# The last down-projection block by thirds of the tokens, with the final norm of finished tiles between its matmuls

## The chip, the cores and the metric

One core of one Trainium2 chip runs the whole program in one launch. The metric is the device time of that core in microseconds; lower is better. Engines are named as in the profile: PE is TensorE, PEld its weight loads, DVE VectorE, ACT ScalarE, POOL GpSimd, SP the queue that issues the DMAs.

## The reference, cut to what matters

One layer of a decoder trunk on 1024 prompt tokens and 8 sample sequences of 4 tokens, all in fp32: two token mixers, then a SwiGLU feed-forward, then a last RMSNorm. The end of it is what the change touches:

```python
h2 = _rmsnorm(x, g_norm2) * (1.0 + scale2) + shift2
ffn = (jax.nn.silu(h2 @ w_ffn_gate) * (h2 @ w_ffn_up)) @ w_ffn_down
x = x + gate2 * ffn
...
y_prompt = _rmsnorm(xp, g_final)
y_sample = _rmsnorm(xs, g_final)
```

x has 1056 rows (tokens) of 1024, w_ffn_gate and w_ffn_up are 1024 x 2816, w_ffn_down is 2816 x 1024. gate2 is one vector for the prompt and one for each of the 8 sample sequences.

## The kernel before, in words

**Layout.** Through the feed-forward phase (`ffn_phase`, from line 1436) everything stands turned: X is 128 partitions x 8 groups of channels (n) x 1056 tokens. The 1056 tokens go by thirds of 352 (`span(c)`, c = 0 to 2), one PSUM bank each. The prompt fills tokens 0 to 1023, the samples the last 32.

**Precision.** Each fp32 matrix is split in a hi and a lo part, and a product is three matmuls: hi by hi, hi by lo, lo by hi. Activations are split when they are made. A weight is loaded into `raw` (SP, line 1613), ScalarE copies the hi part (`hi`, line 1726), GpSimd subtracts it for the lo part (`lo`, line 1795). These go by halves through rings of four slots: half k waits for its load, and for its slot to be used up (`s_used`, three halves back), and tells TensorE by `s_lo`.

**Blocks.** The 2816 inner channels go in 11 blocks of 256. A block has a "proj" step (gate and up) and a "down" step. `run` (line 1520) puts them in order: proj 0, then in a loop proj and down in turn, each down one block behind, and last down of block 10 by itself. So the last two steps are down 9 and down 10. A down step has four halves of weights. Halves 0 and 1 are the two groups of 128 inner channels for output channels n = 0 to 3, halves 2 and 3 the same for n = 4 to 7. Before the first 12 pieces TensorE waits for halves 0 and 1, before the other 12 for 2 and 3:

```python
for nh in range(2):
    sl = []
    for f in range(2):
        s, _, before = pl.half(2 * nh + f)
        pe.wait_ge(s_lo, before + 1)
        sl.append(s)
    for r in range(12):
        n, c = r // 3, r % 3
        bnk, turns = pl.piece(12 * nh + r)
        wait(pe, s_pf[bnk], turns)
```

A piece is one n and one third c: six matmuls of 352 columns (line 1675) into one of banks 0 to 3, which take turns. The step counts itself used (`s_used`) when its piece 11 or 23 is done, both halves at once. All four slots of the rings are in use in a down step, so half k of one down step stands in the slot of half k of the down step ahead of it where no proj lies between, as for blocks 9 and 10.

**Updates.** VectorE adds each piece to X (`add_prompt`, line 1912: X + gate2 * bank, 352 columns, or 320 for the last third) and frees the bank (`s_pf`). For the last third the 32 sample columns come first, in two small operations (`samples`, lines 1920 and 1923).

**The end.** When the last piece is in X, nine token tiles (eight of 128 tokens, one of 32) are turned back, normed and stored. Tile t: eight transposes into two banks (line 1717, TensorE), two squares with a sum over the row (line 1783, ScalarE), the mean square (lines 1957 and 1958, VectorE), the root (line 1787, ScalarE), the reciprocal and two products with g_final (`rows_out`, lines 1929 and 1935, VectorE) into one of four row buffers, and a store (line 1621 or 1623, SP). The eight banks make four pairs, so tile t waits for the products of tile t - 4. ScalarE's order is written out: the squares of tile t, then the root of tile t - 1. VectorE's is the mean square of tile t, then the products of tile t - 1. Roots use a table of ScalarE's, which is loaded ahead of the first of them (ACT_TABLE_LOAD).

Of the kernel before, what the change touches and what calls it, by code (L numbers as in the profile page):

```python
# [9 lines left out]
ALU = mybir.AluOpType  # L10
ACT = mybir.ActivationFunctionType


P = 128
D = 1024
# [13 lines left out]
EPS = 1e-6  # L29
# [1406 lines left out]
def ffn_phase(nc, g, a, loops=True):  # L1436

    with ExitStack() as ctx:
# [124 lines left out]

        def wait_full(e, kind, pl, k):

            if kind == "down":
                nh, r = k // 12, k % 12
                if r == 11:
                    e.wait_ge(s_used, pl.half(2 * nh + 1)[2] + 1)
                else:  # L1570
                    e.wait_ge(s_piece, pl.full(11 * nh + r) + 1)
            else:
                t, c = k // 3, k % 3
                if c == 2:
                    e.wait_ge(s_used, pl.half(2 * t + 1)[2] + 1)
                else:
                    e.wait_ge(s_piece, pl.full(2 * t + c) + 1)

        MISC = g.ps[4:8]
        ENDB = g.ps[4:8] + g.ps[0:4]  # L1580
        NE = len(ENDB) // 2
        PARTS = [(0, 512), (512, 512), (SEQ, NS)]
        seqv = lambda v: v.rearrange("p (b t) -> p b t", t=SLEN)

        with nc.Block() as block:
# [43 lines left out]
            def _(pe):  # L1629
# [24 lines left out]
                def step(kind, b, par, pl):  # L1654
                    if kind == "out":
                        tile3(pl, 0, mix=(b == 0))
                    elif kind == "proj":
                        for t in range(4):
                            tile3(pl, t, first=(t == 0 and isinstance(b, int) and b == 0))
                    elif kind == "down":  # L1660
                        pe.wait_ge(s_al, b * 6 + 6)
                        for nh in range(2):
# [9 lines that stand above are left out]
                                c0, w = span(c)  # L1672
                                for f in range(2):
                                    for m, (x, y) in enumerate(((Wh, Ah), (Wh, Al), (Wl, Ah))):
                                        last = pe.matmul(g.ps[bnk][:, 0:w], x[:, sl[f], n, :], y[:, par, f, c0:c0 + w],  # L1675
                                                         start=(f == 0 and m == 0), stop=(f == 1 and m == 2))
                                if r == 11:
                                    last.then_inc(s_used, 2)
                                else:
                                    last.then_inc(s_piece, 1)  # L1680
                    elif kind == "norm2":

                        pe.wait_ge(s_sq, KC - 1)
                        pe.wait_ge(s_sql, 1)
                        pe.wait_ge(s_cc, 2)
                        for b, (c0, m) in enumerate(PARTS):
                            pe.matmul(MISC[b][0:1, 0:m], g.ones[:, 0:1], SQ[:, c0:c0 + m], start=True, stop=False)  # L1687
                            pe.matmul(MISC[b][0:1, 0:m], g.ones[:, 0:1], SG[:, c0:c0 + m], start=False, stop=True).then_inc(s_row, 1)  # L1688
                        pe.wait_ge(s_rowc, len(PARTS))
                        for t in range(NT):  # L1690
                            n = P if t < NC else NS
                            last = pe.transpose(MISC[3][0:n, 64 + 2 * t:65 + 2 * t], TH[0:1, t * P:t * P + n], g.ident[0:1, 0:1])
                        last.then_inc(s_sum, 1)

                        pe.wait_ge(s_rd, 1)
                        for b, (c0, m) in enumerate(PARTS):
                            n = P if b < 2 else NS
                            pe.matmul(MISC[b][:, 0:m], g.ones[0:n, :], SQ[0:n, c0:c0 + m], start=True, stop=True).then_inc(s_rb, 1)  # L1698


                for half_ in range(2):
                    for k in range(4):
                        kk = 4 * half_ + k
                        last = pe.transpose(MISC[half_][0:KEEP, k * P:(k + 1) * P], g.pk[:, kk, :], g.ident[:, :])
                pe.transpose(MISC[2][0:H * NCOND, 0:P], g.nout[:, :], g.ident[:, :]).then_inc(s_co, 1)
                run(pe, step)

                lastp = Place(LOOP, None, 0)
                bnk, turns = lastp.piece(23)
                pe.wait_ge(s_pf[bnk], turns + 1)  # L1710
                for t in range(NT):
                    n = P if t < NC else NS
                    for b in range(2):
                        if t >= NE and b == 0:
                            pe.wait_ge(s_fo, t - NE + 1)
                        for k in range(4):
                            last = pe.transpose(ENDB[2 * (t % NE) + b][0:n, k * P:(k + 1) * P], X[:, 4 * b + k, t * P:t * P + n], g.ident[:, :])
                        last.then_inc(s_ft, 1)

            @block.scalar  # L1720
            def _(act):
# [54 lines left out]
                for t in range(NT + 1):  # L1776
                    n = P if t < NC else NS
                    for b in range(2):
                        if t < NT:
                            act.wait_ge(s_ft, 2 * t + b + 1)  # L1780
                            if 2 * t + b:
                                act.wait_ge(s_fs, 2 * t + b)
                            act.activation(TH[0:n, 0:512], ENDB[2 * (t % NE) + b][0:n, :], ACT.Square,  # L1783
                                           accum_out=fss[0:n, t, b:b + 1]).then_inc(s_fs, 1)
                    if t:
                        act.wait_ge(s_fm, t)
                        act.activation(fss[:, t - 1, 2:3], fss[:, t - 1, 2:3], ACT.Sqrt).then_inc(s_fr, 1)
# [52 lines left out]
            def _(dve):  # L1840
# [3 lines left out]
                def step(kind, b, par, pl):  # L1844
# [37 lines left out]
                    elif kind == "proj":  # L1882
                        for f in range(2):
# [7 lines left out]
                            for c in range(NPC):  # L1891
                                c0, w = span(c)
                                bnk, _ = pl.piece(6 * f + 3 + c)
                                gb, gt = pl.piece(6 * f + c)
                                wait_full(dve, "proj", pl, 6 * f + 3 + c)
                                dve.wait_ge(s_pf[gb], gt + 1)
                                wait(dve, s_al, n - 3 + (c + 1))
                                dve.scalar_tensor_tensor(AC[:, c0:c0 + w], SG[:, c0:c0 + w], 0.5, g.ps[bnk][:, 0:w],  # L1898
                                                         ALU.mult, ALU.mult).then_inc(s_pf[bnk], 1)
                    else:  # L1900
                        for k in range(24):
                            n, c = 4 * (k // 12) + k % 12 // 3, k % 3
# [12 lines left out]
                def samples(kind, pl, k, n, vec, count):  # L1915
# [6 lines left out]
                    dve.wait_ge(s_stm, count * 2 - 1)  # L1922
                    dve.tensor_tensor(X[:, n, SEQ:T], X[:, n, SEQ:T], stm[:, :], ALU.add).then_inc(s_stm, 1)

                def rows_out(t):

                    n = P if t < NC else NS
                    dve.wait_ge(s_fr, t + 1)
                    link(dve.reciprocal(fss[:, t, 3:4], fss[:, t, 2:3]))
                    if t == 0:  # L1930
                        dve.wait_ge(s_out, 16 * 4)
                    if t >= NXR:
                        dve.wait_ge(s_y[t % NXR], 16 * (t // NXR))
                    for b in range(2):
                        ins = dve.scalar_tensor_tensor(OT[0:n, t % NXR, 512 * b:512 * b + 512], ENDB[2 * (t % NE) + b][0:n, :], fss[0:n, t, 3:4],  # L1935
                                                       GF[0:n, 512 * b:512 * b + 512], ALU.mult, ALU.mult)
                    ins.then_inc(s_fo, 1)

# [10 lines left out]
                    dve.wait_ge(s_mh, m + 1)  # L1949
                    dve.tensor_tensor(g.Hl[:, m, :], mixed(m), g.Hh[:, m, :].bitcast(F32), ALU.subtract).then_inc(s_mlv, 1)  # L1950
                run(dve, step)
                dve.wait_ge(s_gf, 16)
                for t in range(NT + 1):
                    if t < NT:
                        n = P if t < NC else NS
                        dve.wait_ge(s_fs, 2 * t + 2)
                        link(dve.tensor_tensor(fss[0:n, t, 2:3], fss[0:n, t, 0:1], fss[0:n, t, 1:2], ALU.add))
                        dve.tensor_scalar(fss[:, t, 2:3], fss[:, t, 2:3], 1.0 / D, EPS, ALU.mult, ALU.add).then_inc(s_fm, 1)
                    if t:
                        rows_out(t - 1)  # L1960


class Shared:
# [68 lines left out]
```

## Time and profile before

| | |
|---|---|
| median of three runs | 2223.32 us (2222.83, 2223.32, 2227.84) |
| span of the profiled execution | 2216.5 us |
| its own time | not listed apart; the median is 6.8 us above the span, the fastest run 6.3 |
| PE busy | 2073.8 us, 94% |
| DVE, ACT, POOL busy | 37%, 26%, 27% |
| mean granted clock of PE | 0.959 |
| last down step's first matmul | at 2169.24 us |
| last piece's update of X ends | at 2193.29 us |
| first products for y | at 2198.80 us |

Times inside the profile are microseconds from the first instruction. In the timeline's rows a start and a length stand first, then the engine and the line, the operation with the tile that it writes and those it reads, the shapes, and how many of such are merged; a bracket names the idle time ahead and what ended it. In the windows view each stretch has its length, then the busy time of each engine with its count of instructions, then PEclk, the granted clock of TensorE as a share of 2.4 GHz, the share of the DMA engines and GB/s. The chain is the work that ended last, followed back from the end.

### The profile page before, as it was taken

How to read it: one execution, taken by the hardware profiler on the slowest of the kernel's cores; microseconds unless marked ns; L12 is line 12 of the kernel's file. 1: busy time of each engine (PE TensorE's matmuls, PEld its weight loads, DVE VectorE, ACT ScalarE, POOL GpSimd, SP SyncE). 2: the span in 40 equal slices, each digit the busy share in tenths (PEclk: the TensorE clock that was granted, in tenths of full speed). 3: DMA queues.
4: the chain of work that ended last, by engine and by line, in shares of the span. 5: the costliest groups of instructions: out<-in, count | busy, mean ns of one | idle time of the engine just before them, and what ended most of it. 6: DMA issues, size and time to landing. Idle time of an engine off the chain costs nothing. (4 is left out here: it accounts for less than half of the span.)

```text
span 2216.5 us, 33043 instructions
## 1 busy us (share of the span) xinstructions
PE 2073.8 (94%) x12501; PEld 1956.4 (88%) x12501; DVE 820.3 (37%) x1494; ACT 570.6 (26%) x1164; POOL 598.4 (27%) x481
## 2 busy tenths in 40 slices
PE   8589999999999999999998889499999999999997
PEld 3589889899898898998998779399999999999997
DVE  4551165320552314634036332613323333233326
ACT  3332233322333133232333220211121112111122
POOL 3311133121231212322113065333322233222330
PEclk9789999989999999999998989699999999999999
DMA  7211222121211312213123151011111111111111
GB/s 243 105 56 45 69 63 53 51 88 52 84 48 34 110 43 60 72 48 98 48 60 102 56 181 39 10 48 48 48 40 48 49 48 44 44 48 49 46 50 79
DMA packets 193052, 144.52 MB, mean 65 GB/s; under 512 B 9396, under 2 KB 178548, under 8 KB 191872
## 3 DMA queue, kind: packets, MB, share of 16 engines
q1 hardware_dynamic: 192896, 142.32, 21.5%
q8 instruction: 113, 1.85, 0.3%
q14 instruction: 43, 0.35, 0.1%
HBM read 119.75 MB, written 22.54 MB: 64 GB/s over the span
## 5 line engine op out<-in xcount | busy, mean ns | idle before, releaser
L773 PE MATMUL bank<-h_hi,w_hi 128*128 128x352 f32 x1560 | 535.1, 343 | 31.0 <-POOL w_lo L1089 24.0
L773 PE MATMUL bank<-h_lo,w_hi 128*128 128x352 f32 x1560 | 515.1, 330 | 0.0
L773 PE MATMUL bank<-h_hi,w_lo 128*128 128x352 f32 x1560 | 514.1, 330 | 0.0
L1647 PE MATMUL bank<-h_hi,f_hi 128*128 128x352 f32 x1248 | 405.3, 325 | 41.2 <-issue 22.2
L1089 POOL TENSOR_TENSOR w_lo<-w_raw,w_hi 128x512 fp32r<-128x512 f32 x130 | 179.8, 1383 | 836.3 <-ACT w_hi L930 828.3
L1647 PE MATMUL bank<-h_lo,f_hi 128*128 128x352 f32 x1248 | 404.4, 324 | 0.0
L1647 PE MATMUL bank<-h_hi,f_lo 128*128 128x352 f32 x1248 | 404.4, 324 | 0.0
L773 PEld LDWEIGHTS bank<-h_hi,w_hi 128*128 128x128 f32 x1560 | 303.1, 194 | 47.1 <-POOL w_lo L1089 23.4
L1795 POOL TENSOR_TENSOR f_lo<-w_raw,f_hi 128x512 fp32r<-128x512 f32 x148 | 190.2, 1304 | 427.4 <-ACT f_hi L1726 427.3
L773 PEld LDWEIGHTS bank<-h_lo,w_hi 128*128 128x128 f32 x1560 | 303.2, 194 | 1.0
L773 PEld LDWEIGHTS bank<-h_hi,w_lo 128*128 128x128 f32 x1560 | 302.2, 194 | 0.0
L1647 PEld LDWEIGHTS bank<-h_hi,f_hi 128*128 128x128 f32 x1248 | 236.3, 189 | 43.1 <-issue 43.1
L1647 PEld LDWEIGHTS bank<-h_lo,f_hi 128*128 128x128 f32 x1248 | 236.2, 189 | 0.0
L1647 PEld LDWEIGHTS bank<-h_hi,f_lo 128*128 128x128 f32 x1248 | 236.1, 189 | 0.0
L1912 DVE SCALAR_TENSOR_TENSOR x_t<-bank,ada,x_t 128x352 f32<-128x352 f32 (+1 forms) x288 | 161.3, 570 | 99.6 <-PE bank L1647 63.9
L1675 PE MATMUL bank<-act_hi,f_hi 128*128 128x352 f32 x528 | 170.2, 322 | 0.0
L1675 PE MATMUL bank<-act_lo,f_hi 128*128 128x352 f32 x528 | 170.0, 322 | 0.0
L1675 PE MATMUL bank<-act_hi,f_lo 128*128 128x352 f32 x528 | 170.0, 322 | 0.0
L1726 ACT ACTIVATE f_hi<-w_raw 128x512 fp32r<-128x512 f32 x148 | 85.7, 622 | 271.1 <-PE bank L1675 196.0
L930 ACT ACTIVATE w_hi<-w_raw 128x512 fp32r<-128x512 f32 x130 | 81.1, 624 | 165.2 <-PE bank L773 154.8
L1889 DVE SCALAR_TENSOR_TENSOR early<-early,bank 128x352 f32<-128x352 f32 x66 | 34.6, 524 | 229.7 <-ACT early L1758 229.7
L1898 DVE SCALAR_TENSOR_TENSOR early<-early,bank 128x352 f32<-128x352 f32 x66 | 34.4, 522 | 209.6 <-PE bank L1647 194.1
(332 smaller groups left out, 2398.1 us busy)
## 6 DMA issues: line engine op xcount, KB each, us to landing
w_raw<-in_w_in SPq DMA_DIRECT2D x128, 256.0 KB, 2.8
w_ada_tile<-in_w_ada SPq DMA_DIRECT2D x32, 512.0 KB, 3.9
w_raw<-in_w_ffn_gate SPq DMA_DIRECT2D x44, 256.0 KB, 3.1
w_raw<-in_w_ffn_up SPq DMA_DIRECT2D x44, 256.0 KB, 3.0
w_raw<-in_w_ffn_down SPq DMA_DIRECT2D x44, 256.0 KB, 2.6
w_ada_ring<-in_w_ada SPq DMA_DIRECT2D x8, 1024.0 KB, 5.2
x_scratch<-x_turned_rows SPq DMA_DIRECT2D x1, 4224.0 KB, 12.7
x_t<-x_scratch SPq DMA_DIRECT2D x4, 1056.0 KB, 11.2
```

The costliest lines, as they stand in the source:

```text
L773: last = pe.matmul(g.ps[b][:, 0:n], x[:, s, k, :], y[:, 4 * h + k, c0:c0 + n], start=(h == 0 and k == 0 and m == 0), stop=(h == 1 and k == ...
L930: act.activation(Wh[:, s], raw[:, r], ACT.Copy).then_inc(s_hi, 1)
L1089: pool.tensor_tensor(Wl[:, s], raw[:, r], Wh[:, s].bitcast(F32), ALU.subtract).then_inc(s_lo, 1)
L1647: last = pe.matmul(g.ps[bnk][:, 0:n], x[:, s, kk, :], y[:, 4 * h + kk, c0:c0 + n], start=(h == 0 and kk == 0 and m == 0), stop=(h == 1 and ...
L1675: last = pe.matmul(g.ps[bnk][:, 0:w], x[:, sl[f], n, :], y[:, par, f, c0:c0 + w], start=(f == 0 and m == 0), stop=(f == 1 and m == 2))
L1726: act.activation(Wh[:, s], raw[:, s], ACT.Copy).then_inc(s_hi, 1)
L1795: pool.tensor_tensor(Wl[:, s], raw[:, s], Wh[:, s].bitcast(F32), ALU.subtract).then_inc(s_lo, 1)
L1889: dve.scalar_tensor_tensor(SG[:, c0:c0 + w], TH[:, c0:c0 + w], 1.0, g.ps[bnk][:, 0:w], ALU.add, ALU.mult).then_inc(s_pf[bnk], 1)
L1898: dve.scalar_tensor_tensor(AC[:, c0:c0 + w], SG[:, c0:c0 + w], 0.5, g.ps[bnk][:, 0:w], ALU.mult, ALU.mult).then_inc(s_pf[bnk], 1)
L1912: dve.scalar_tensor_tensor(X[:, n, c0:c0 + m], g.ps[bnk][:, 0:m], g.ada[:, vec + n, 0:1], X[:, n, c0:c0 + m], ALU.mult, ALU.add).then_inc( ...
```

## The change

The step of block 10 gets code of its own. TensorE waits for all four halves ahead of its first matmul. Its 24 pieces go by thirds, the outer loop being the token third (c = r // 8), the inner the channel group n. Each piece signals by `s_piece`. After pieces 9, 11, 17, 19 and 22 TensorE transposes token tiles 0 to 4, each once the piece that completes its tokens is in X (piece 7 for tiles 0 and 1, piece 15 for tiles 2 to 4) and, from tile 2 on, once its banks are free. Tiles 0 to 4 use bank pairs of banks 4 to 7 in turn; tiles 5 and 6 get banks 0 to 3, tiles 7 and 8 wait for the products of tiles 3 and 4. VectorE does the mean squares of tiles 0 to 3 after its pieces 12, 14, 19 and 21, and the products after its pieces 13, 15, 20 and 22. The loops at the end begin at tile 5 (transposes) and tile 4 (mean square). ScalarE's order of squares and roots stays as it is, and so does SP's of the stores.

The diff, without the lines that only rename a bank:

```diff
@@ wait_full
-            if kind == "down":
+            if kind == "last":
+                e.wait_ge(s_piece, pl.full(k) + 1)
+            elif kind == "down":
...
         MISC = g.ps[4:8]
         ENDB = g.ps[4:8] + g.ps[0:4]
-        NE = len(ENDB) // 2
+        TURN_BANKS = [0, 1, 0, 1, 0, 2, 3, 1, 0]
+        BEFORE_IT = [None, None, 0, 1, 2, None, None, 3, 4]
+        TURN_AFTER = {9: (0,), 11: (1,), 17: (2,), 19: (3,), 22: (4,)}
+        MS_AFTER = {12: (0,), 14: (1,), 19: (2,), 21: (3,)}
+        ROWS_AFTER = {13: (0,), 15: (1,), 20: (2,), 22: (3,)}
+
+        def endb(t, b):
+            return ENDB[2 * TURN_BANKS[t] + b]
...
@@ TensorE
+                    elif kind == "down" and is_last(b):
+                        pe.wait_ge(s_al, b * 6 + 6)
+                        for k in range(4):
+                            pe.wait_ge(s_lo, pl.half(k)[2] + 1)
+                        for r in range(24):
+                            c, n = r // KC, r % KC
+                            bnk, turns = pl.piece(r)
+                            wait(pe, s_pf[bnk], turns)
+                            c0, w = span(c)
+                            for f in range(2):
+                                s = pl.half(2 * (n // 4) + f)[0]
+                                for m, (x, y) in enumerate(((Wh, Ah), (Wh, Al), (Wl, Ah))):
+                                    last = pe.matmul(g.ps[bnk][:, 0:w], x[:, s, n % 4, :], y[:, par, f, c0:c0 + w],
+                                                     start=(f == 0 and m == 0), stop=(f == 1 and m == 2))
+                            last.then_inc(s_piece, 1)
+                            for t in TURN_AFTER.get(r, ()):
+                                turn_out(t, pl)
...
+                def turn_out(t, pl):
+
+                    n = P if t < NC else NS
+                    bnk, turns = pl.piece(KC * ((min(T, (t + 1) * P) - 1) // PC + 1) - 1)
+                    pe.wait_ge(s_pf[bnk], turns + 1)
+                    if BEFORE_IT[t] is not None:
+                        pe.wait_ge(s_fo, BEFORE_IT[t] + 1)
+                    for b in range(2):
+                        for k in range(4):
+                            last = pe.transpose(endb(t, b)[0:n, k * P:(k + 1) * P], X[:, 4 * b + k, t * P:t * P + n], g.ident[:, :])
+                        last.then_inc(s_ft, 1)
...
-                lastp = Place(LOOP, None, 0)
-                bnk, turns = lastp.piece(23)
-                pe.wait_ge(s_pf[bnk], turns + 1)
-                for t in range(NT):
...
+                for t in range(5, NT):
+                    turn_out(t, Place(LOOP, None, 0))
@@ VectorE
+                    elif is_last(b):
+                        for k in range(24):
+                            c, n = k // KC, k % KC
+                            if c == NPC - 1:
+                                samples("last", pl, k, n, 5 * KC, b * KC + (KC + n + 1))
+                            add_prompt("last", pl, k, n, c, 5 * KC)
+                            for t in MS_AFTER.get(k, ()):
+                                mean_square(t)
+                            for t in ROWS_AFTER.get(k, ()):
+                                rows_out(t)
...
+                def mean_square(t):
+
+                    n = P if t < NC else NS
+                    dve.wait_ge(s_fs, 2 * t + 2)
+                    link(dve.tensor_tensor(fss[0:n, t, 2:3], fss[0:n, t, 0:1], fss[0:n, t, 1:2], ALU.add))
+                    dve.tensor_scalar(fss[:, t, 2:3], fss[:, t, 2:3], 1.0 / D, EPS, ALU.mult, ALU.add).then_inc(s_fm, 1)
...
-                dve.wait_ge(s_gf, 16)
-                for t in range(NT + 1):
...
+                for t in range(4, NT):
+                    mean_square(t)
+                    if t > 4:
+                        rows_out(t - 1)
+                rows_out(NT - 1)
```

## Rows read from the trace of the kernel before

**Rows 1.** The page's first line: span and instructions.
```profile
span 2216.5 us, 33043 instructions
```

**Rows 2.** Chain that ended last, from 2146 us: start, length, what.
```profile
2146.39 45.98 PE bank L1675 x288
...
2192.82 0.47 DVE x_t L1912
...
2194.03 0.70 ACT early L1783 x2
...
2198.80 1.41 DVE y_rows L1935 x2
...
2200.57 1.41 DVE y_rows L1935 x2
```

**Rows 3.** Timeline of the tail: start, length, engine, line, operation [idle before].
```profile
2193.33 3.71 PE L1717 MATMUL bank<-identity,x_t 128*128 128x128 f32 x32 [0.97 <-DVE x_t L1912]
...
2194.80 0.60 ACT L1783 ACTIVATE early<-bank 128x512 f32<-128x512 f32 x1
...
2195.59 0.16 DVE L1957 TENSOR_TENSOR final_small<-final_small 128x1 f32<-128x1 f32 x1 [2.32 <-ACT early L1783]
2195.79 0.15 DVE L1958 TENSOR_SCALAR final_small<-final_small 128x1 f32<-128x1 f32 x1
...
2198.60 0.16 DVE L1929 RECIPROCAL final_small<-final_small 128x1 f32<-128x1 f32 x1 [1.17 <-ACT final_small L1787]
...
2212.68 1.40 DVE L1935 SCALAR_TENSOR_TENSOR y_rows<-bank,final_small,early 32x512 f32<-32x512 f32 x2
```

**Rows 4.** Timeline at the start of the last block: TensorE, ScalarE, GpSimd.
```profile
2169.24 0.32 PE L1675 MATMUL bank<-act_hi,f_hi 128*128 128x352 f32 x1
...
2169.49 1.15 ACT L1726 ACTIVATE f_hi<-w_raw 128x512 fp32r<-128x512 f32 x2 [10.38 <-PE bank L1675]
...
2170.20 2.54 POOL L1795 TENSOR_TENSOR f_lo<-w_raw,f_hi 128x512 fp32r<-128x512 f32 x2 [8.98 <-ACT f_hi L1726]
```

**Rows 5.** Matmuls after idle time (timeline of PE), and the clock of that stretch (windows).
```profile
735.72 0.66 PE L773 MATMUL bank<-h_hi,w_hi 128*128 128x352 f32 x1 [3.49 <-issue]
...
739.04 0.32 PE L773 MATMUL bank<-h_hi,w_lo 128*128 128x352 f32 x1
...
735.52:738.93 3.41, 3.21 (x11) 0.50 0.40 163
...
1201.79 0.66 PE L773 MATMUL bank<-h_hi,w_hi 128*128 128x352 f32 x1
...
1206.62 0.32 PE L773 MATMUL bank<-h_lo,w_hi 128*128 128x352 f32 x1
```

**Rows 6.** Eight transposes of an earlier stage, timeline of PE.
```profile
438.59 1.07 PE L909 MATMUL bank<-identity,v_b 128*128 128x128 f32 x8
```

**Rows 7.** VectorE's updates of X, timeline around 2170 us.
```profile
2169.54 0.19 DVE L1920 TENSOR_TENSOR sample_temp<-bank,ada 128x32 f32<-128x32 f32 x1 [0.48 <-PE bank L1675]
...
2169.88 1.09 DVE L1912 SCALAR_TENSOR_TENSOR x_t<-bank,ada,x_t 128x320 f32<-128x320 f32 x2
2171.34 0.58 DVE L1912 SCALAR_TENSOR_TENSOR x_t<-bank,ada,x_t 128x352 f32<-128x352 f32 x1 [0.37 <-PE bank L1675]
```

**Rows 8.** ScalarE's table loads and what followed them, timeline.
```profile
1431.18 1.28 ACT L1758 ACT_TABLE_LOAD   x1
1435.90 0.47 ACT L1758 ACTIVATE early<-bank 128x352 f32<-128x352 f32 x1 [3.44 <-PE bank L1647]
...
2197.07 1.28 ACT L1787 ACT_TABLE_LOAD   x1
...
2198.36 0.20 ACT L1787 ACTIVATE final_small<-final_small 128x1 f32<-128x1 f32 x1
```

**Rows 9.** Windows in the tail, TensorE transposing alone; PEclk is the granted clock.
```profile
2200.26:2203.25 2.99, 2.99 (x14) 2.79 (x15) 2.85 (x10) 2.75 (x11) 0.00 (x0) 0.50 0.57 233
2203.25:2208.10 4.85, 3.39 (x27) 2.61 (x26) 4.64 (x15) 4.45 (x16) 0.00 (x0) 1.00 0.71 289
```

More of the change, by code:

```diff
@@ L1706, in _ @@
                 run(pe, step)
-                lastp = Place(LOOP, None, 0)
-                bnk, turns = lastp.piece(23)
-                pe.wait_ge(s_pf[bnk], turns + 1)
-                for t in range(NT):
[L1712 to L1718, printed above, removed]
+                for t in range(5, NT):
+                    turn_out(t, Place(LOOP, None, 0))
             @block.scalar
@@ L1782, in _ @@
                                 act.wait_ge(s_fs, 2 * t + b)
-                            act.activation(TH[0:n, 0:512], ENDB[2 * (t % NE) + b][0:n, :], ACT.Square,
+                            act.activation(TH[0:n, 0:512], endb(t, b)[0:n, :], ACT.Square,
                                            accum_out=fss[0:n, t, b:b + 1]).then_inc(s_fs, 1)
@@ L1930, in rows_out @@
                     if t == 0:
+                        dve.wait_ge(s_gf, 16)
                         dve.wait_ge(s_out, 16 * 4)
@@ L1934, in rows_out @@
                     for b in range(2):
-                        ins = dve.scalar_tensor_tensor(OT[0:n, t % NXR, 512 * b:512 * b + 512], ENDB[2 * (t % NE) + b][0:n, :], fss[0:n, t, 3:4],
+                        ins = dve.scalar_tensor_tensor(OT[0:n, t % NXR, 512 * b:512 * b + 512], endb(t, b)[0:n, :], fss[0:n, t, 3:4],
                                                        GF[0:n, 512 * b:512 * b + 512], ALU.mult, ALU.mult)
@@ L1951, in _ @@
                 run(dve, step)
-                dve.wait_ge(s_gf, 16)
-                for t in range(NT + 1):
[L1954 to L1959, printed above, removed]
+                for t in range(4, NT):
+                    mean_square(t)
+                    if t > 4:
                         rows_out(t - 1)
+                rows_out(NT - 1)
 class Shared:
```

## The prediction

> **What bounds the kernel now.** The page gives a span of 2216.5 us [rows 1]; the median of the three runs is 2223.32, 6.8 more (the fastest, 2222.83, is 6.3 more). The profiled execution's own time is not listed, so I work every change against the span and add it to the median. I read the chain that ended last first, because the change touches only the end: the chain holds 288 matmuls of line 1675 without a hole for 45.98 us from 2146.39, that is the last two down blocks, 144 matmuls each, 0.160 us apart. So TensorE bounds the last block until 2192.35. Then nothing of TensorE matters: the last update of X ends at 2193.29, the first y rows are written from 2198.80, one tile every 1.77 us (2198.80 to 2200.57) by VectorE, and the last rows end at 2214.08 [rows 2, 3], the span at 2216.5. From the last X update to the end 23.2 us pass in which TensorE only transposes. That is what the change goes for.
>
> **The gain behind the matmuls.** Four tiles (0 to 3) leave the tail and tile 4 is transposed ahead. After the last X update: transposes start 0.06 later, their first half is full 0.67 later (2193.33 to 2194.03), the two squares run 0.78 apart (2194.03, 2194.80) and the second is done 0.70 after its start: 2.24 [rows 2, 3]. VectorE's mean square starts 0.08 on, and in program order it stands ahead of tile 4's rows: 0.35 to its result, beside which the reciprocal starts, 0.20 from there to the first product, 1.41 for two. ScalarE takes tile 4's root, which stands behind tile 5's squares, within that. Tile 4's rows end 4.2 after the last X update. Tiles 5, 6, 7 follow at 1.77 (ScalarE's own pace of two squares and a root is 1.6, the transposes lie beside), the small one takes 1.5: 11.0, and 2.4 for the last store as now: 13.4 instead of 23.2. **Gain 9.8.**
>
> **Cost 1, the start of the block.** The new code waits for all four halves of the weights before its first matmul. Halves 2 and 3 go into slots of a ring of four that the block before reads until its last matmul. The trace shows it: TensorE starts the last block at 2169.24 and ScalarE begins the two splits at 2169.49, having waited 10.38 for TensorE; GpSimd's two lo parts run 2170.20 to 2172.74 [rows 4]. Now this lies under the first 72 matmuls, which use halves 0 and 1. Then the first matmul starts at 2172.80: **3.56 lost**, whole, since nothing else is there for TensorE. The loads landed long before; no queue is passed.
>
> **Cost 2, the clock.** After an idle time of 3.49 us the matmuls from 735.72 on run at a granted clock of 0.50 (1.2 GHz): 11 of them take until 739.04, 3.32 us where 0.160 each would be 1.76 [rows 5]. So 1.56 is lost. The stall here is as long, and I take it once. Lower bound 0 (the clock stays at 2.4 GHz, or the low stretch lies in the idle time); upper bound 2.27, from the stretch at 1201.79, where 16 matmuls take 4.83 us instead of 2.56 [rows 5].
>
> **Cost 3, transposes between matmuls.** 40 are moved ahead (5 tiles of 8). The trace of before has no transposes inside this stream; the nearest are the tail's own, 32 in 3.71 us, 0.93 for eight [rows 3], and eight of an earlier stage among other work, 1.07 [rows 6]. I take 1.01 a tile, 5.05 in all, since between matmuls they are nearer to the second; bounds 0.93 and, for a change of kind on either side, 1.2 (an estimate: 1.07 and what 1.07 is over 0.93).
>
> **Cost 4, waits between the engines.** This is the part that a sum of durations misses, so I walk the chain.
> - TensorE fills piece 13 after 84 matmuls, 13.41, two tiles of transposes, 2.02, the clock, 1.56, and 0.16 by which the last matmul outlasts its slot: 2189.95. VectorE's update (0.05 + 0.58) [rows 7] ends at 2190.6. Tile 0's root is ready by then: its mean square follows piece 12, and ScalarE's table load of 1.28 was issued ahead of the wait. At 1431.18 such a load runs at once though its activation waits until 1435.90 [rows 8]. Were it behind the wait, 0.9 would come on top.
> - The y rows of tile 0 (0.20 + 1.41), piece 14, mean square 1 (0.30), piece 15: 2193.65.
> - Then VectorE stops. The y rows of tile 1 stand behind piece 15 and need root 1; ScalarE runs it behind the squares of tile 2; these need tile 2's transposes, which TensorE starts when piece 15 is in X (it finishes piece 17 at 2193.7 too). So 0.06 + 0.67 + 0.03 + 0.78 + 0.70, the root 0.10 and the y rows 1.64: 2197.63. Queued behind the waiting y rows are the updates of pieces 16 to 19, and behind those TensorE's banks and tile 3's transposes.
> - From there VectorE has no slack. Pieces of the last third carry the samples: 0.34 + 0.53, some 0.84 in a row [rows 7]; eight are 6.72. Two mean squares 0.6, two row steps 3.22, 0.4 of waiting for root 3 (behind the squares of tile 4, whose transposes wait for the y rows of tile 2): 10.94. Last X update 2208.57. TensorE is done with its matmuls some 3 us earlier; before, it was 1.
>
> **Sum.** 2208.57 + 13.4 = 2222.0 for the span, +5.5; in pieces: -9.8, +3.56, +1.56, +5.05, and 5.1 for waits. The stores of tiles 0 to 3 move ahead of the end, and SP's queue has nothing behind them but the other stores: nothing. Banks 4 to 7 are free since norm2: nothing. Predicted time 2223.32 + 5.5 = **2228.8**, 0.25% slower, which is within 0.3%, about what a measurement of this kernel can tell from no change.
>
> Weighed against it: the Trainium skill, ScalarE: Activation LUTs, "What ACT_TABLE_LOAD costs", adds a drain of about 1380 ns to each load of 1283 ns. The rows show the 1.28 but no drain: the load starts at 2197.07, straight behind the squares, and the root at 2198.36 [rows 8]. By the page tile 0's rows would be 1.2 later and the time 2230.0; I go by the rows.
>
> **Rivals.**
> A, slower: **the low clock lasts longer or comes twice.** TensorE idles again ahead of tiles 3 and 4 (about 1 and 2 us). For it: a low stretch reached from 1201.79 over 16 matmuls until 1206.62, longer than the one that I take [rows 5]. Against it: these matmuls have VectorE as their bound, which covers part. Price 0.7 (2.27 for 1.56) to 2.3 (a second stretch of 1.56 on top): 2229.5 to 2231.1, typically 2230.8. It decides once more than 1.2 us of it fall ahead of piece 17, where TensorE carries the chain.
> The Trainium skill, TensorE: Matmul & The Clock Gate, "Part 4: PE-mode transpose", says that transposes do not count as busy for the clock, which would make A the rule, at 2230.8. The trace speaks against it: from 2200.26 on TensorE ran nothing but transposes, and the clock rose from 0.50 to 1.00 at about 2203.25 [rows 9].
> B: **the stall at the start does not come**, the splits being done in time. 5.1 less: 2223.7. Nothing in the rows speaks for it.
> C: **VectorE's order costs nothing**, TensorE is the bound to the end. Last X update 2172.80 + 23.0 + 5.05 + 1.56 + 1.1 = 2203.5, time 2223.7; half of the waits gives 2226. For it: VectorE's work on the last third, 10.5, is no more than TensorE's 10.7 there.
> D: **both B and C**, the plain reading of the change: -9.8 + 5.05 = -4.7, 2218.6. Even that is no 0.3%; faster by more would need transposes that are free.
>
> **How the numbers follow.** Forecast 0.58 (its own range 2227 to 2231; 0.18 of it above 2230.0, for terms that I set too low), A 0.20, B 0.08, C 0.12, D and better 0.02. Slower by over 0.3% (above 2230.0) is 0.18 + 0.20 = 0.38; faster by over 0.3% (below 2216.7) gets all of D's 0.02; the rest is 0.60. The range goes from 2224.0 to 2232.5: it takes in A, the upper bounds, and half of the way to B and C.
>
> **What would show it.** A hole of 3.5 us ahead of the last block's first matmul, released by GpSimd's f_lo, and a clock of 0.50 behind it, in the windows view; VectorE's rows of tile 1 waiting 2.4 us for ScalarE; the last X update some 15 us later than 2193.3; five row steps behind it at 1.77; 13.4 from there to the end. No hole at the start makes it B. TensorE busy until 1 us ahead of the last X update makes it C. A second stretch at 0.50 ahead of 2193 is A.

## The result and the profile after

The changed kernel takes 2229.33 us (median of 13 runs, 2227.26 to 2232.88) against 2223.96 for the kernel before (13 runs, 2218.09 to 2227.84). The ratio is 1.0024, 95% interval 1.0017 to 1.0031: 5.4 us slower, outside the noise of this comparison, and under the 0.3% that the prediction set as its line.

The spans of the two profiled executions differ by more: 2216.5 and 2227.4. Of these 10.9 us, 5.0 lie ahead of the code that changed. Block 9's last matmul leaves its slot at 2169.24 before [rows 4] and at 2174.20 after (it starts at 2174.03, and 0.16 on the next one could). The profiled execution after has a time of its own, 2229.13, which is 1.7 above its span. In every run on record that has its span beside it the two differ by 1.7 to 1.8. So the profiled execution of before took about 2218.2 (an estimate: its span and 1.7), as fast as the fastest of its 13 runs, 2218.09. So one profile's span says little about 5 us here, and everything below is measured by the **end part**, from the moment at which block 9's last matmul leaves its slot to the end of the span: 47.26 us before, 53.20 after, 5.9 more.

The first fence is the windows view of the changed kernel's end part. Its columns are the stretch, its length, then busy time and count of PE, PEld, DVE, ACT and POOL, then the granted clock, the DMA share and GB/s.

```profile
2174.20:2177.16 2.96, 0.15 (x1) 0.00 (x0) 0.84 (x3) 1.15 (x2) 2.01 (x2) 1.00 0.00 0
2177.16:2180.57 3.41, 2.68 (x9) 2.71 (x10) 0.54 (x1) 0.00 (x0) 0.48 (x1) 0.50 0.02 5
2180.57:2183.99 3.42, 3.42 (x14) 3.42 (x13) 1.07 (x3) 0.00 (x0) 0.00 (x0) 0.50 0.00 0
2183.99:2190.48 6.49, 6.49 (x43) 6.47 (x42) 3.64 (x7) 0.00 (x0) 0.00 (x0) 1.00 0.00 0
2190.48:2200.00 9.52, 9.52 (x67) 9.42 (x66) 5.92 (x14) 4.24 (x10) 0.00 (x0) 1.00 0.08 34
2200.00:2214.05 14.05, 8.64 (x59) 7.84 (x57) 11.11 (x38) 4.51 (x15) 0.00 (x0) 1.00 0.23 90
2214.05:2227.40 13.35, 5.38 (x32) 5.01 (x32) 8.56 (x26) 6.05 (x21) 0.00 (x0) 0.65 0.53 206
```

Read it from the top. TensorE is idle at first; at 2177.16, in the idle time still, the granted clock falls to 0.50 (1.2 GHz) and stays there until 2183.99; then TensorE is full at 2.4 GHz until 2200; from there to the last X update it is busy for only 8.64 of 14.05. The last stretch, from that update to the end, is the tail: 13.35 instead of the 23.2 of before. Of those 9.9, 7.1 are the four row steps of 1.77 that are gone. The other 2.8 are the start: the first y rows stand 2.70 behind the last update (2216.75) and no longer 5.53, mostly because in the kernel before tile 1's squares (2195.58 to 2197.05) and the table load of 1.28 [rows 8] stood ahead of tile 0's root.

The timeline of the changed kernel shows the start of the block, which answers to [rows 4]; both splits stand in one row:

```profile
2174.45 1.15 ACT L1755 ACTIVATE f_hi<-w_raw 128x512 fp32r<-128x512 f32 x2 [10.39 <-PE bank L1701]
...
2175.15 2.49 POOL L1824 TENSOR_TENSOR f_lo<-w_raw,f_hi 128x512 fp32r<-128x512 f32 x2 [8.98 <-ACT f_hi L1755]
...
2177.89 0.63 PE L1681 MATMUL bank<-act_hi,f_hi 128*128 128x352 f32 x1 [3.54 <-POOL f_lo L1824]
2178.32 0.49 PE L1681 MATMUL bank<-act_lo,f_hi 128*128 128x352 f32 x1
```

The hole is 3.54 us and GpSimd's lo part ends it. The chain that ended last, in the changed kernel (start, length, what), then shows which work set the end in the middle of the block:

```profile
2177.89 12.59 PE bank L1681 x60
2190.48 0.87 PE bank L1736 x8
2191.35 1.91 PE bank L1681 x12
2193.26 0.87 PE bank L1736 x8
2194.14 5.73 PE bank L1681 x36
2199.86 0.46 PE bank L1736 x4
...
2201.94 0.17 DVE final_small L1975
...
2208.51 0.75 DVE y_rows L1982
...
2209.40 0.64 PE bank L1736 x4
```

Ten pieces, tile 0's transposes (0.87 on the chain), two pieces, tile 1's, six pieces: TensorE sets the pace down to the first half of tile 2's transposes. There the chain leaves TensorE for ScalarE and VectorE and comes back only for transposes. The two waits that do it, in the timeline of VectorE and ScalarE:

```profile
2201.72 0.19 ACT L1816 ACTIVATE final_small<-final_small 128x1 f32<-128x1 f32 x1
...
2201.94 0.16 DVE L1975 RECIPROCAL final_small<-final_small 128x1 f32<-128x1 f32 x1 [2.34 <-ACT final_small L1816]
2202.14 1.41 DVE L1982 SCALAR_TENSOR_TENSOR y_rows<-bank,final_small,early 128x512 f32<-128x512 f32 x2
...
2211.66 0.16 DVE L1975 RECIPROCAL final_small<-final_small 128x1 f32<-128x1 f32 x1 [0.56 <-ACT final_small L1816]
...
2213.51 0.54 DVE L1951 SCALAR_TENSOR_TENSOR x_t<-bank,ada,x_t 128x320 f32<-128x320 f32 x1
```

VectorE stands 2.34 us ahead of tile 1's y rows and 0.56 ahead of tile 3's, both for ScalarE's root. The last X update ends at 2214.05, that is 39.85 after block 9; before it was 24.03 [rows 2, 4]. So the last update comes 15.8 later and the tail is 9.9 shorter.

### The profile page after: what moved, and what is told of

It is laid out like the page before. It is cut to its first block and busy times, and to the rows that moved or that the text cites. A ratio compares the mean times of both kernels' runs of the same rounds, so it can differ in the third digit from the quotient of the medians.

```text
span 2227.4 us, 33047 instructions
## 1 busy us (share of the span) xinstructions
PE 2079.3 (93%) x12501; PEld 1961.0 (88%) x12501; DVE 820.4 (37%) x1494; ACT 570.8 (26%) x1164; POOL 598.6 (27%) x481
## 5 line engine op out<-in xcount | busy, mean ns | idle before, releaser
L1701 PE MATMUL bank<-act_hi,f_hi 128*128 128x352 f32 x480 | 154.7, 322 | 0.0
L1701 PE MATMUL bank<-act_hi,f_lo 128*128 128x352 f32 x480 | 154.6, 322 | 0.0
L1701 PE MATMUL bank<-act_lo,f_hi 128*128 128x352 f32 x480 | 154.5, 322 | 0.0
```

## The experiments

Seven kernels, all one edit or two away from the changed one. The end part and its two pieces are from the profile of one execution each: from block 9's end to the end of the last X update, and from there to the end of the span. Block 9's end is 0.25 ahead of ScalarE's first split of halves 2 and 3, as in [rows 4]. The ratio is against the kernel before, run beside each group: its median was 2223.96 beside the change, 2225.90 beside e1, e2, e4 and e5, and 2225.22 beside e3, e6 and e7. The intervals are wide against these effects (that of e5 overlaps that of the change), so the readings below rest on the profiles, and the times only agree with them.

| kernel | ratio, 95% interval | end part | to the last X update | from there |
|---|---|---|---|---|
| before | 1 | 47.26 | 24.03 | 23.23 |
| the change | 1.0024 (1.0017 to 1.0031) | 53.20 | 39.85 | 13.35 |
| e1_late_wait | 0.9999 (0.9989 to 1.0008) | 46.58 | 33.29 | 13.29 |
| e2_roots_first | 1.0001 (0.9987 to 1.0015) | 49.09 | 35.73 | 13.36 |
| e4_thirds_only | 1.0023 (1.0013 to 1.0032) | 53.78 | 30.54 | 23.24 |
| e5_warm_wait | 1.0014 (1.0004 to 1.0024) | 51.05 | 37.21 | 13.84 |
| e3_both | 0.9986 (0.9977 to 0.9995) | 43.98 | 30.38 | 13.60 |
| e6_thirds_late | 0.9999 (0.9990 to 1.0008) | 47.19 | 23.96 | 23.23 |
| e7_rows3_last | 0.9974 (0.9963 to 0.9985) | 42.67 | 29.33 | 13.34 |

### e1_late_wait: wait for halves 2 and 3 where they are read

```diff
-                        for k in range(4):
+                        for k in range(2):
                             pe.wait_ge(s_lo, pl.half(k)[2] + 1)
                         for r in range(24):
+                            if r == 4:
+                                for k in range(2, 4):
+                                    pe.wait_ge(s_lo, pl.half(k)[2] + 1)
```

> The changed kernel, but TensorE waits for halves 2 and 3 of the weights only ahead of piece 4, the first that reads them. I measure by the end part: from the moment at which block 9's last matmul leaves its slot to the end of the span; 47.3 us before, 53.2 after the change. Theory 1 (the early wait costs the idle time and, through it, the clock): no hole, clock 1.00 through the block, piece 9 done 6.5 us sooner after block 9 than with the change (3.54 idle and 3.0 of slow matmuls), and the whole chain behind it moves along: end part 46.7, time about 0.3% under the changed kernel. Theory 2 (only the idle time itself counts, the slow matmuls are hidden by VectorE's chain): end part 49.7.

The end part is 46.58, as theory 1 has it (46.7). The windows view of this kernel, from block 9's end to tile 0's transposes:

```profile
2171.42:2180.95 9.53, 9.53 (x61) 9.52 (x61) 6.07 (x12) 1.15 (x2) 2.55 (x2) 1.00 0.01 2
```

Ten pieces in 9.53 us without a gap and at clock 1.00, where the changed kernel needs 3.69 and 12.43. The last X update comes 6.56 sooner, the tail is the same. So nothing of the slow matmuls was hidden, and theory 2 falls. Four pieces later is enough: piece 4 starts 3.8 us after piece 0, and GpSimd's lo parts end 3.5 after it.

### e2_roots_first: each early tile's root behind its own squares

```diff
+                for t in range(4):
+                    squares_of(t)
+                    root_of(t)
+                squares_of(4)
+                for t in range(5, NT):
+                    squares_of(t)
+                    root_of(t - 1)
+                root_of(NT - 1)
```

`squares_of` and `root_of` hold the lines that were in ScalarE's loop.

> The changed kernel, but ScalarE takes the root of each of tiles 0 to 3 straight behind its squares, not behind the next tile's; from tile 4 on the order is as it was. Theory 1 (VectorE stands at tile 1's y rows until root 1, which is queued behind the squares of tile 2): VectorE's waits for roots 1 and 3 go, the last X update is 2.5 us sooner after block 9, end part 50.7. Theory 2 (TensorE is the bound up to the last piece, VectorE's wait is slack): end part stays at 53.2 within 0.3. The hole at the start and the low clock stay as they are in both.

The end part is 49.09, 1.6 under theory 1's 50.7. Most of that is not this edit's: the low clock was shorter in this execution. The windows of the changed kernel, from the first matmul to tile 0's transposes, and of this one:

```profile
2177.89:2190.32 12.43, 12.43 (x61) 12.41 (x62) 5.25 (x9) 0.00 (x0) 0.00 (x0) 0.75 0.01 1
```

```profile
2178.31:2189.49 11.18, 11.18 (x61) 11.16 (x61) 5.25 (x9) 0.00 (x0) 0.00 (x0) 0.85 0.01 1
```

The clock fell at 2178.51 here, behind the first matmul, and was back at 2181.93. That is 1.25 of the 4.1 us gained. The other 2.9 belong to the roots, for which 2.5 was expected; e3_both against e1_late_wait, where neither has a low clock in the block, gives the same 2.9 (33.29 less 30.38). Tile 1's y rows now start at 2198.77 in VectorE's timeline, 20.46 after the block's first matmul; with the change it was 24.25. Of these 3.8, 1.25 are the clock again:

```profile
2198.58 0.16 DVE L1984 RECIPROCAL final_small<-final_small 128x1 f32<-128x1 f32 x1
2198.77 1.41 DVE L1991 SCALAR_TENSOR_TENSOR y_rows<-bank,final_small,early 128x512 f32<-128x512 f32 x2
```

The bracket with an idle time is gone. So VectorE's wait was on the path, and theory 2 falls.

### e4_thirds_only: the thirds without the early tiles

```diff
-        TURN_BANKS = [0, 1, 0, 1, 0, 2, 3, 1, 0]
-        BEFORE_IT = [None, None, 0, 1, 2, None, None, 3, 4]
-        TURN_AFTER = {9: (0,), 11: (1,), 17: (2,), 19: (3,), 22: (4,)}
-        MS_AFTER = {12: (0,), 14: (1,), 19: (2,), 21: (3,)}
-        ROWS_AFTER = {13: (0,), 15: (1,), 20: (2,), 22: (3,)}
+        TURN_BANKS = [0, 1, 2, 3, 0, 1, 2, 3, 0]
+        BEFORE_IT = [None, None, None, None, 0, 1, 2, 3, 4]
+        TURN_AFTER = {23: (0, 1, 2, 3, 4)}
+        MS_AFTER = {23: (0,)}
+        ROWS_AFTER = {}
```

All transposes wait for piece 23, and VectorE's last loop begins at tile 1.

> The changed kernel without its early tiles: the block goes by thirds and waits for all four halves, but transposes, mean squares and y rows of all nine tiles run behind the last piece in the order and banks of the kernel before. Theory 1 (the wait at the start costs 3.5 us and the clock 1.6 to 3.0): end part 47.3 + 3.5 + 3.0 = 53.8, so the early tiles earn no more than 1 us net in the changed kernel, since what they take off the tail goes into transposes and waits. Theory 2 (the thirds cost nothing, the early tiles are what is slower): end part 47.3.

The end part is 53.78, the expected 53.8. The windows of this kernel: hole, block, tail.

```profile
2176.82:2180.52 3.70, 0.16 (x2) 0.04 (x1) 0.85 (x3) 1.15 (x2) 2.49 (x2) 0.90 0.00 0
2180.52:2207.36 26.84, 25.93 (x144) 25.64 (x144) 16.11 (x40) 0.00 (x0) 0.00 (x0) 0.89 0.00 1
2207.36:2230.60 23.24, 10.25 (x72) 8.86 (x72) 15.55 (x46) 14.57 (x46) 0.00 (x0) 0.79 0.47 187
```

The tail is back at 23.24, and the block costs 6.5 more than before. So in the changed kernel the early tiles earn 53.78 - 53.20 = 0.6 us: they take 9.9 off the tail and put 9.3 into the block. In the times even that does not show (1.0023 against 1.0024).

### e5_warm_wait: matmuls with no use in the hole

```diff
-                        for k in range(4):
+                        for k in range(2):
                             pe.wait_ge(s_lo, pl.half(k)[2] + 1)
+                        for m in range(21):
+                            pe.matmul(g.ps[7][:, 0:PC], Wh[:, pl.half(0)[0], m % 4, :], Ah[:, par, 0, 0:PC], start=True, stop=True)
+                        for k in range(2, 4):
+                            pe.wait_ge(s_lo, pl.half(k)[2] + 1)
```

> The changed kernel, with 21 more matmuls of 352 columns on weights and activations that are there, into bank 7 which nothing reads, between the waits for halves 0 and 1 and those for halves 2 and 3. They fill 3.4 of the 3.54 us of idle time and add nothing to the result. Theory 1 (the idle time lets the clock fall): clock 1.00 through the block, the first ten pieces take 9.6 us instead of 12.6, end part 50.2. Theory 2 (the low clock comes from something else, the order of the block or its waits): a stretch at 0.50 stays and the end part stays at 53.2.

This parts the hole from the clock, since piece 0 starts as late as with the change. The windows of this kernel, up to piece 0 and from there to tile 0's transposes:

```profile
2176.25:2179.86 3.61, 3.52 (x22) 3.25 (x22) 0.85 (x3) 1.15 (x2) 2.55 (x2) 1.00 0.00 0
2179.86:2189.62 9.76, 9.76 (x61) 9.74 (x62) 5.26 (x9) 0.00 (x0) 0.00 (x0) 1.00 0.01 2
```

The clock stays at 1.00 and the ten pieces take 2.67 less than in the changed kernel. The last X update comes 2.64 sooner. So here the idle time is what lets the clock fall, and what it costs goes through to the last X update undiminished. The other profiles agree: the three with the hole (the change, e2, e4) have a low stretch at the start of the block, the five without it (before, e1, e3, e6, e7) have none. The end part is 51.05 and not 50.2: 0.4 because 2.6 and not 3.0 came back, and 0.5 in the tail. In this execution the clock fell at 2212.96, 0.56 ahead of the transposes of tile 5, and the eight of them hold the chain for 1.98; with the change it fell at 2214.7, 0.6 behind their start, and they hold it for 1.45.

### e3_both, e6_thirds_late and e7_rows3_last

e3_both has the edits of e1 and e2 together. e6_thirds_late has those of e4 and e1. e7_rows3_last is e3_both with one number changed:

```diff
-        ROWS_AFTER = {13: (0,), 15: (1,), 20: (2,), 22: (3,)}
+        ROWS_AFTER = {13: (0,), 15: (1,), 20: (2,), 23: (3,)}
```

> The changed kernel with both edits: the late wait for halves 2 and 3, and the roots of tiles 0 to 3 straight behind their squares. By the same end part (47.3 before, 53.2 changed, 46.6 with the late wait alone): theory 1, the two costs add up, so what e2 took off comes off here too: end part 44.0, some 0.15% faster than the kernel before. Theory 2, TensorE's bound takes over once the clock stays up, and VectorE's wait becomes slack: end part stays near 46.6.

> The thirds alone, without early tiles, with the late wait for halves 2 and 3. Theory 1 (the wait is all that the thirds cost): end part 47.3, the same as the kernel before. Theory 2 (going by thirds costs something of its own, since all samples updates stand in the last third): end part 48 or more.

> The kernel with both edits, and the y rows of tile 3 behind piece 23 rather than piece 22, where VectorE otherwise stands 2.7 us waiting for tile 5's squares. Theory 1 (VectorE's queue sets the last X update): the last X update 1.6 us sooner than with both edits, the tail as long as there, end part 42.3, about 0.2% faster than the kernel before. Theory 2 (TensorE's matmuls and transposes, 23.0 + 4.4, already set the last update): end part within 0.4 of the kernel with both edits.

**e3_both** came out at 43.98 (expected 44.0), and the time at a ratio of 0.9986. The two costs add: 6.6 for the wait, 2.6 more for the roots. Up to the last X update the roots are worth 2.9; 0.3 goes back in the tail, where the clock fell 0.35 behind the start of tile 5's transposes and they hold the chain for 1.69. **e6_thirds_late** at 47.19 is the kernel before (47.26) within 0.1. Going by thirds costs nothing by itself, though the small samples updates then stand in eight pieces running. All of the 6.6 us between e4 (53.78) and e6 are the wait. **e7_rows3_last** missed its number: 42.67, expected 42.3. The last X update came 1.05 sooner than in e3_both, not 1.6, so theory 1 holds in kind and only for two thirds. What is left is a wait of TensorE's for a bank pair, in its timeline:

```profile
2197.24 1.03 PE L1739 MATMUL bank<-identity,x_t 128*128 128x128 f32 x8
...
2201.82 1.06 PE L1739 MATMUL bank<-identity,x_t 128*128 128x128 f32 x8 [0.66 <-DVE y_rows L1994]
...
2204.82 2.84 PE L1739 MATMUL bank<-identity,x_t 128*128 128x128 f32 x24 [0.97 <-DVE x_t L1963]
```

Tile 4 waits 0.66 for the y rows of tile 2. Ahead of the tail TensorE now waits 0.97 for the last X update, exactly what it was in the kernel before [rows 3]; with the change it was 2.67. So TensorE is the bound again up to the last piece, but for that 0.66. The timeline of VectorE in this kernel shows where the y rows of tile 3 went:

```profile
2204.86 1.41 DVE L1994 SCALAR_TENSOR_TENSOR y_rows<-bank,final_small,early 128x512 f32<-128x512 f32 x2
2207.01 0.16 DVE L1980 TENSOR_TENSOR final_small<-final_small 128x1 f32<-128x1 f32 x1 [0.48 <-ACT early L1814]
```

They start 0.1 after the last X update at 2204.76, in time in which VectorE waits for tile 5's squares anyway. In e3_both that wait was 2.24, here it is 0.48, and the tail is 13.34, no longer than with the change. This kernel has the lowest ratio of all, 0.9974 (0.9963 to 0.9985), though its interval overlaps that of e3_both. By the ratio it is 5.8 us faster than the kernel before; the medians differ by 4.6, as do the end parts.

## Why the prediction was right

Predicted were 2228.8 us and a loss of 5.5; measured were 2229.33 and 5.4. The range held, and the change stayed inside 0.3%, the likeliest of the three cases. The mechanism is the one forecast. That the two numbers agree to 0.1 is luck: the interval of the ratio is 3.8 to 6.9 us, and misses of about +1.4 and -0.9 on the way to the last X update stand against each other (39.33 after block 9's end by the walk, 39.85 measured). The way there, step by step against the profile after (times after the block's first matmul or the last X update):

- **The gain of the tail**, 9.8: measured 23.23 - 13.35 = 9.9. Tile 4's rows were to end 4.2 after the last update (the terms given add to 4.28); they end at 2218.16, 4.1 after. A low clock from 2214.7 to 2218.1 cost nothing there: in e7, where the clock stays at 1.00 through these transposes, the tail is 13.34.
- **Cost 1**, a hole of 3.56 from block 9's last slot to the first matmul, ended by GpSimd: measured 3.69 (2174.20 to 2177.89), of which the timeline calls 3.54 idle, with the releaser as named. e1 shows that all of it counts, e4 and e6 that it and the clock are all that the thirds cost.
- **Cost 2**, the clock, 1.56 and at most 2.27: this is the term that was mis-sized. The ten pieces took 12.43 us up to tile 0's transposes, where 60 times 0.160 is 9.6: 2.8 lost, above the upper bound (e5, with the hole filled, gives back 2.7). With the 3.69 of the hole that is 6.5, and e1 gets 6.56 back. The low stretch lasted until 2183.99, 6.1 us into the block. In the row that I priced it by it had covered 3.3 us of matmuls. The row behind the upper bound, at 1201.79 [rows 5], was misread: it stands in the middle of a low stretch and not behind idle time. The timeline and the windows of the kernel before show 2.23 of idle time ahead of 1198.78, and a stretch as long as the one that came:

```profile
1198.78 2.83 PE L862 MATMUL bank<-q_decayed,k_decayed 128*128 128x64 f32 x16 [2.23 <-DVE q_decayed L1263]
...
1199.78:1206.61 6.83, 6.83 (x27) 6.65 (x27) 5.05 (x6) 2.22 (x4) 3.88 (x2) 0.50 0.00 0
```

  With that stretch under matmuls of this block the bound would have been some 3.1 (an estimate: 6.83 at 0.293 a matmul is 23 of them, 0.133 lost on each). e2's execution lost 1.3 less, so this term moves from run to run. It is rival A's mechanism (the low clock lasts longer), at its place ahead of piece 17. Other terms that came out smaller made up for part of it. Cause and price are shown by e5: with the hole filled the clock did not fall.
- **Cost 3**, 1.01 us a tile: 0.87 on the chain. 0.3 less over the two tiles that stand ahead of piece 17. It is less than in the kernel before's tail, 0.93; a change of kind between matmuls and transposes shows no cost.
- **Cost 4**, the walk. y rows of tile 1 done 24.83 after the first matmul: measured 25.66, the clock's 1.3 more, less the transposes' 0.3 and 0.2 of small steps. VectorE's wait for root 1 is 2.34 in the profile; the walk has 2.37, from the end of piece 15 to the reciprocal. From there to the last X update 10.94: measured 10.50, as updates that queue up follow at 0.78 and not 0.84 (2203.46 to 2204.25). e2 confirms the cause that the walk named: not VectorE's own work, but the root queued behind the squares of a tile that is not there yet.
- **The table load** was to lie ahead of the wait with no drain. It starts at 2195.22 straight behind the squares, ahead of the mean square that the root waits for (2195.82). The root ends at 2196.72 and the update of piece 13 at 2196.67, so the load costs VectorE 0.2 at most. The Trainium skill's drain of about 1380 ns (ScalarE: Activation LUTs, "What ACT_TABLE_LOAD costs") does not show here either:

```profile
2195.22 1.28 ACT L1816 ACT_TABLE_LOAD   x1
2196.52 0.20 ACT L1816 ACTIVATE final_small<-final_small 128x1 f32<-128x1 f32 x1
...
2196.75 0.17 DVE L1975 RECIPROCAL final_small<-final_small 128x1 f32<-128x1 f32 x1
```

- **Rival A by the Trainium skill** (TensorE: Matmul & The Clock Gate, "Part 4: PE-mode transpose": transposes do not count as busy for the clock): through the block, from 2183.99 to 2214.05 with five tiles of transposes and idle times of 1.02 and 1.77 us ahead of two of them, the clock stays at 1.00 in the windows. That does not bear out a second fall, though the stretch has more matmuls than transposes and so is a weak test of the rule.
- **Rivals B and C.** The hole came, and TensorE ran out ahead of the last update by 2.7, so neither holds for the change. e1 is B made true: 6.6 us, not the 5.1 priced, again the clock. e7 is nearly B and C together, and D's sum of -4.7 is met by its -4.6 in the end part (-9.9 in the tail, +5.3 up to the last X update).
- **The 6.8 us between the profiled span and the median** were left unexplained. About 1.7 of them are what a run takes beyond its span; the rest is spread between runs, as the profiled execution was one of the shortest. It cost nothing, since only the difference was carried over.

Not settled: what sets how long the clock stays low. After the same hole it was 6.83 us with the change and in e4, where it fell in the idle time, and 3.4 in e2, where it fell behind the first matmul. No run isolates the 0.66 wait of tile 4; a third bank pair could not be had with banks 0 to 3 in use by the pieces, and it was not tried.

## What to carry to other kernels

A reordered loop reads its weights in another order, so ask of each wait that moves to the front which buffer it fills and who still reads that buffer; here one wait for two halves too many cost 6.6 us, more than the 4.6 that the early tiles gain in the best of these kernels. When work of several engines is threaded into a stream, every engine's written-out order must be threaded too: a root that stood harmlessly behind the next tile's squares in a dense tail holds up the whole queue of updates once that tile comes microseconds later (2.9 us here). And put work that nothing waits for into the stretch where its engine idles anyway: moving one step of 1.6 us behind the last piece was worth 1 us.

## What the runs showed of the hardware

In an idle time of 3.54 us the granted clock fell to 0.50 and stayed there for 6.83 us in one execution of the changed kernel, and the matmuls, 0.160 apart at full clock, were 0.29 apart. In the execution of e2, after the same idle time, it was low for 3.4 us. With the idle time filled by 21 matmuls of 352 columns there was no low stretch. Eight transposes between fp32 matmuls held the chain for 0.87 us, less than the 0.93 that eight of the 32 take in the tail of the kernel before, with no cost of changing over that the timeline shows. ScalarE's table load of 1.28 us started ahead of the wait of the root that needed it, and no drain followed it.
